# Down-projections of a split-precision FFN: three 256-column matmuls per weight tile, or one of 512 columns and one of 256

## The reference

```python
FFN_HIDDEN = 2816        # 22 chunks of 128
D_FF = 3 * D_MODEL       # 3072: 24 chunks of 128

# first block
gt, up = jnp.split(h @ w_gate_up[i], 2, axis=-1)
f = (jax.nn.silu(gt) * up) @ w_down[i]                        # (256, 2816) @ (2816, 1024)
x = x + rms_norm(f, ffn_post_g[i])

# second block
u = causal_dwconv(jnp.einsum('bsd,df->bsf', h, w_up[l]), ffn_conv_w[l])
gate, up = jnp.split(u, 2, axis=-1)
x = x + jnp.einsum('bsf,fd->bsd', jax.nn.gelu(gate) * up, w_down[l])   # (256, 3072) @ (3072, 1024)
return rms_norm_2(x, final_g)
```

## Time and profile before

| | us |
|---|---|
| median of 3 runs | 949.2 (949.17 to 949.22) |
| the profiled execution, whole time | 949.5 |
| its span, first to last instruction | 947.7 |
| PE busy | 935.1 (99% of the span) |
| PE weight loads (PEld), beside the matmuls | 905.7 (96%) |
| DVE busy | 720.0 (76%) |
| ACT busy | 523.2 (55%) |
| POOL busy | 17.1 (2%) |
| first down-projection on PE | 521.96 to 586.25 |
| second down-projection on PE | 867.63 to 937.68 |

### The profile page before, as it was taken

The page is one execution under the profiler, slowest core; times in us unless marked ns, Lnnn a source line. Parts: engine busy times, 40 slices in busy tenths (PEclk is TensorE's granted clock), DMA queues, the critical chain, the costliest instruction groups (busy, mean ns, idle before and its releaser), DMA issues.

```text
span 947.7 us, 19332 instructions
## 1 busy us (share of the span) xinstructions
PE 935.1 (99%) x7228; PEld 905.7 (96%) x7228; DVE 720.0 (76%) x1297; ACT 523.2 (55%) x871; POOL 17.1 (2%) x27
## 2 busy tenths in 40 slices
PE   9999999999999999999999999999999999999997
PEld 7999999999999999999999999999988999999997
DVE  5999999999999888677767445898615888888432
ACT  5547666777667475555554434577213656656331
POOL 0000000000000000000000000000000000000001
PEclk9999999999999999999999999999999999999999
DMA  7576334544544557256555555346046555555601
GB/s 303 181 247 204 127 120 170 199 154 157 193 130 165 201 197 239 98 189 234 179 186 186 174 184 178 112 158 198 25 154 221 192 185 179 181 187 182 204 0 45
DMA packets 45324, 161.54 MB, mean 170 GB/s; under 512 B 5172, under 2 KB 6360, under 8 KB 45144
## 3 DMA queue, kind: packets, MB, share of 16 engines
q1 hardware_dynamic: 43200, 154.61, 48.5%
q10 hardware_dynamic: 2072, 6.21, 1.9%
HBM read 159.72 MB, written 1.09 MB: 170 GB/s over the span
## 4 chain that ended last, share of the span: by engine, by line
PE 63%; issue 24%; DVE 9%; ACT 2%; DMA 1%; POOL 0%; DVEq 0%; ACTq 0%; SPq 0%; POOLq 0%
PE A L393 11%; PE A L394 10%; PE A L395 10%; PE B L393 5%; PE B L395 5%; PE B L394 5%; PE B L588 5%; PE B L755 3%; DVE w_lo L1191 2%; DVE part L1227 2%; PE B L743 1%; DVE acc L1430 1%; ACT dec L906 1%; PE A L569 1%; DMA raw<-in_weights_dram 1%
## 5 line engine op out<-in xcount | busy, mean ns | idle before, releaser
L1191 DVE TENSOR_TENSOR w_lo<-raw,w_hi 128x1024 fp32r<-128x1024 f32 x257 | 312.8, 1222 | 98.2 <-ACT w_hi L804 95.9
L804 ACT ACTIVATE w_hi<-raw 128x1024 fp32r<-128x1024 f32 x257 | 268.8, 1054 | 134.6 <-PE B L395 75.1
L393 PE MATMUL A<-h_lo,w_hi 128*128 128x256 f32 x1176 | 338.0, 287 | 3.2 <-DVE h_lo L1586 1.6
L394 PE MATMUL A<-h_hi,w_hi 128*128 128x256 f32 x1176 | 332.8, 283 | 0.0
L395 PE MATMUL A<-h_hi,w_lo 128*128 128x256 f32 x1176 | 332.8, 283 | 0.0
L393 PEld LDWEIGHTS A<-h_lo,w_hi 128*128 128x128 f32 x1176 | 225.3, 192 | 6.0 <-issue 3.8
L394 PEld LDWEIGHTS A<-h_hi,w_hi 128*128 128x128 f32 x1176 | 225.5, 192 | 0.2
L395 PEld LDWEIGHTS A<-h_hi,w_lo 128*128 128x128 f32 x1176 | 225.3, 192 | 0.0
L393 PE MATMUL B<-h_lo,w_hi 128*128 128x256 f32 x448 | 128.0, 286 | 0.4 <-DVE h_lo L1196 0.4
L394 PE MATMUL B<-h_hi,w_hi 128*128 128x256 f32 x448 | 126.8, 283 | 0.0
L395 PE MATMUL B<-h_hi,w_lo 128*128 128x256 f32 x448 | 126.8, 283 | 0.0
(11 more groups left out here) (243 smaller groups left out, 1093.8 us busy)
## 6 DMA issues: line engine op xcount, KB each, us to landing
raw<-in_weights_dram SPq DMA_DIRECT2D x290, 512.0 KB, 4.0
csrow<-cs_dram ACTq DMA_DIRECT2D x9, 512.0 KB, 4.2
x<-in_x_dram SPq DMA_DIRECT2D x2, 512.0 KB, 5.1
bd<-in_lru_w_dram ACTq DMA_DIRECT2D x1, 1024.0 KB, 4.8
out_dram<-m_wide SPq DMA_DIRECT2D x5, 128.0 KB, 2.2
out_dram<-m_wide ACTq DMA_DIRECT2D x3, 128.0 KB, 2.3
par<-in_params_dram SPq DMA_DIRECT2D x1, 379.0 KB, 7.3
cst<-in_consts_dram SPq DMA_DIRECT2D x1, 320.0 KB, 7.5
```

Source lines behind the costliest of these rows:

```text
L393: mm(dst, wh, lo, start=first, stop=False, skip_group_check=free)
L394: mm(dst, wh, hi, start=False, stop=False, skip_group_check=free)
L804: F(w_hi[:, s, :], raw[:, s, :], ACT.Copy).then_inc(hi_ready, 1)
L1191: V.tensor_tensor(w_lo[:, s, :], raw[:, s, :], w_hi[:, s, :].bitcast(F32), ALU.subtract).then_inc(lo_ready, 1)
```

## The change

The two halves of the operand lie side by side in one buffer, `hid[:, k, :]` = [lo | hi], 512 columns. For outputs m = 0 to 6 a tile is two matmuls: w_hi on all 512 columns, whose sums with lo land in the left half of a bank and those with hi in the right half, and w_lo on the 256 columns of hi, which adds to the left half. Each of these outputs has a bank of its own, 512 columns of partial sums that have to be added afterwards. Output 7 keeps the three matmuls of 256 columns in the left half of the eighth bank; its right half stays free.

With a bank for each output, the first matmul of each starts the sum, the clearing matmuls go, and the loop of `down_turns` is written out. The banks are taken in the order in which the up-projection's last pairs leave them, with a wait for every second output (`staged` in the first FFN, `pairs_drained` in the second). The waits of PE in the rest, on outputs 0 to 3 before it went on to 4 to 7, go.

The extra addition: in the first FFN, ACT copies the right half to `m_wide` (`half_copied`), DVE adds the left half in place (`m_copied`), and ACT squares the sum. In the second, DVE adds two halves to the residual, one after the other. The norm's scratch columns move from A3 and A2 to banks 1 and 2 of B.

```diff
--- before.py
+++ after.py
@@ -222,8 +222,8 @@
         s3.close()
 
         s4 = ExitStack()
-        hid_hi = sb("hid_hi", [P, KF2, T], F32R, s4)
-        hid_lo = sb("hid_lo", [P, KF2, T], F32R, s4)
+        hid = sb("hid", [P, KF2, 2 * T], F32R, s4)
+        hid_lo, hid_hi = hid[:, :, 0:T], hid[:, :, T:2 * T]
         stage3 = sb("stage3", [P, 2, T], scope=s4)
         s4.close()
 
@@ -279,7 +279,10 @@
 
         DVE_OUT = 5
         out_weighted = stage[:, 0, :], stage[:, 1, :], stage2[:, 0, :]
-        pool_rstd = A[2][:, T:2 * T]
+        pool_rstd = B[:, 2, T:2 * T]
+
+        DOWN_BANKS = [B[:, n, :] for n in (1, 2, 0, 3)] + [A[n][:, :] for n in range(4)]
+        down_sums, down_rstd = B[:, 1, 0:TT], B[:, 1, T:2 * T]
 
         LRU_BANKS = [A[n][:, 0:T] for n in range(3)] + [B[:, n, 0:T] for n in range(4)] + [A[3][:, 0:T]]
         SC_BANKS = [A[0][:, 0:T]] + [B[:, n, 0:T] for n in range(4)] + [A[3][:, 0:T]]
@@ -326,6 +329,7 @@
         lru_tap, sc_ready, lru_ready = sem("lru_tap"), sem("sc_ready"), sem("lru_ready")
         sc_x_used = sem("sc_x_used")
         out_ready, stored = sem("out_ready"), sem("stored")
+        half_copied = sem("half_copied")
         weighted, pool_out = sem("weighted"), sem("pool_out")
         last_scale = sem("last_scale")
 
@@ -661,23 +665,30 @@
             for j in range(UP1_TURNS * 4, KF):
                 ring_pair(j, 0)
 
-            def down_turns(p, turns, operand):
-
-                with pe.Fori(0, turns) as i:
-                    for m in range(KD):
-                        pe.wait_ge(lo_ready, split_order(p + m, i))
-                        if m == 0:
-                            pe.wait_ge(operand_ready, i * 8 + (operand + 8))
-                        for k in range(8):
-                            ins = tile((p + m) % RING, k, hid_hi[:, bass.ds(i * 8 + k, 1), :].rearrange("p a t -> p (a t)"),
-                                       hid_lo[:, bass.ds(i * 8 + k, 1), :].rearrange("p a t -> p (a t)"),
-                                       acc_out(m), False, False, True)
-                        ins.then_inc(pieces_done, 1)
-
-            pe.wait_ge(staged, STAGED_FFN1 + 4 * UP1_TURNS)
-            clear_accumulators()
+            def down_tile(slot, j, k, m, first, last):
+
+                if m == KD - 1:
+                    return tile(slot, j, hid_hi[:, k, :], hid_lo[:, k, :], DOWN_BANKS[m][:, 0:T], first, last, True)
+                wh = w_hi[:, slot, j * P:(j + 1) * P]
+                mm(DOWN_BANKS[m], wh, hid[:, k, :], start=first, stop=False, skip_group_check=True)
+                return mm(DOWN_BANKS[m][:, 0:T], w_lo[:, slot, j * P:(j + 1) * P], hid_hi[:, k, :], start=False, stop=last,
+                          skip_group_check=True)
+
+            def down_turns(p, turns, operand, drained_by_now, drained_n):
+
+                for n in range(turns * KD):
+                    i, m = n // KD, n % KD
+                    pe.wait_ge(lo_ready, split_order(p + n))
+                    if i == 0 and m % 2 == 0:
+                        pe.wait_ge(drained_by_now, drained_n + m // 2)
+                    if m == 0:
+                        pe.wait_ge(operand_ready, i * 8 + (operand + 8))
+                    for k in range(8):
+                        ins = down_tile((p + n) % RING, k, i * 8 + k, m, n < KD and k == 0, False)
+                    ins.then_inc(pieces_done, 1)
+
             done1 = 3 * KD
-            down_turns(DOWN1, 2, done1)
+            down_turns(DOWN1, 2, done1, staged, STAGED_FFN1 + KF - 3)
             for n in range(DOWN1_REST * KD):
                 p = DOWN1 + 2 * KD + n // 8
                 m, k = n // DOWN1_REST, n % DOWN1_REST
@@ -685,13 +696,10 @@
                     pe.wait_ge(lo_ready, split_order(p))
                 if m == 0:
                     pe.wait_ge(operand_ready, done1 + 2 * KD + k + 1)
-                if m >= 4 and k == 0:
-                    pe.wait_ge(m_copied, KD + m - 3)
-                ins = tile(p % RING, n % 8, hid_hi[:, 2 * KD + k, :], hid_lo[:, 2 * KD + k, :], acc_out(m),
-                           False, False, True)
+                ins = down_tile(p % RING, n % 8, 2 * KD + k, m, False, k == DOWN1_REST - 1)
                 if n % 8 == 7:
                     ins.then_inc(pieces_done, 1)
-            spread_residual(5, 13, 4 * KD, A[2][:, :], 2)
+            spread_residual(5, 13, 4 * KD, B[:, 2, :], 2, norm_bank=B[:, 1, :])
 
 
             ops = done1 + KF
@@ -768,21 +776,16 @@
                 for j in range(4):
                     pe.wait_ge(pairs_drained, i * 4 + (KD + j - 3))
                     up2_pair(j, i)
-            pe.wait_ge(pairs_drained, KD + KF2 - 2)
-            clear_accumulators()
-            down_turns(DOWN2, 2, ops + KD)
+            down_turns(DOWN2, 2, ops + KD, pairs_drained, KD + KF2 - 3)
             for m in range(KD):
                 p = DOWN2 + 2 * KD + m
                 pe.wait_ge(lo_ready, split_order(p))
                 if m == 0:
                     pe.wait_ge(operand_ready, ops + KD + KF2)
-                if m >= 4:
-                    pe.wait_ge(x_new, 3 * KD + m - 3)
                 for k in range(8):
-                    ins = tile(p % RING, k, hid_hi[:, 2 * KD + k, :], hid_lo[:, 2 * KD + k, :], acc_out(m), False, False,
-                               True)
+                    ins = down_tile(p % RING, k, 2 * KD + k, m, False, k == 7)
                 ins.then_inc(pieces_done, 1)
-            spread_residual(8, 16, 7 * KD, A[2][:, :], 4, 0)
+            spread_residual(8, 16, 7 * KD, B[:, 2, :], 4, 0, norm_bank=B[:, 1, :])
             for t in range(TT):
                 ins = mm(pool_rstd[:, t * P:(t + 1) * P], scale[:, t:t + 1].to_broadcast([P, P]), ident, start=True, stop=True)
             ins.then_inc(rstd_ready, 1)
@@ -1076,7 +1079,12 @@
                     split_hi(p + LEAD)
 
                 act.wait_ge(pieces_done, down1_done(m))
-                copy_and_square(acc_out(m), m_wide[:, m, :], sq_wide[:, m, 0:T])
+                if m == KD - 1:
+                    copy_and_square(DOWN_BANKS[m][:, 0:T], m_wide[:, m, :], sq_wide[:, m, 0:T])
+                else:
+                    F(m_wide[:, m, :], DOWN_BANKS[m][:, T:2 * T], ACT.Copy).then_inc(half_copied, 1)
+                    act.wait_ge(m_copied, KD + m + 1)
+                    F(sq_wide[:, m, 0:T], m_wide[:, m, :], ACT.Square).then_inc(squares_ready, 1)
 
             act.dma_start(bd[:, :, :, :], lru_w).then_inc(lru_w_loaded, 16)
 
@@ -1665,11 +1673,14 @@
                     split_lo(p + LEAD)
                 if c == 0:
                     lru_rates()
-                if c < KD - 2:
-                    add_square(sq_wide, 4 * KD, c)
-                if c == KD - 3:
+                if c < KD - 1:
+                    dve.wait_ge(half_copied, c + 1)
+                    V.tensor_tensor(m_wide[:, c, :], m_wide[:, c, :], DOWN_BANKS[c][:, 0:T], ALU.add).then_inc(m_copied, 1)
+                if 1 <= c < KD - 1:
+                    add_square(sq_wide, 4 * KD, c - 1)
+                if c == KD - 2:
                     add_squares_up()
-            residual_scaled(14, 13, "ffn_post_g", "norm1_g_2", hi_n, KD, sums, rstd)
+            residual_scaled(14, 13, "ffn_post_g", "norm1_g_2", hi_n, KD, down_sums, down_rstd)
             sum_squares(sq_wide, 5 * KD)
             for p in range(LRUX0 + LEAD, LRUX0 + LEAD + 2):
                 split_lo(p)
@@ -1851,12 +1862,21 @@
             hid2_low(KF2 - 1, 1)
             for p in range(DOWN2, PIECES):
                 split_lo(p + LEAD)
-            add_accumulated(down2_done, 7 * KD)
-            moment_of(17, D, RMS_EPS).then_inc(mean_ready, 1)
+            for m in range(KD):
+                dve.wait_ge(pieces_done, down2_done(m))
+                if m < KD - 1:
+                    after(own.up(V.tensor_tensor(x[:, m, :], x[:, m, :], DOWN_BANKS[m][:, 0:T], ALU.add)))
+                half_ = slice(0, T) if m == KD - 1 else slice(T, 2 * T)
+                V.tensor_tensor(x[:, m, :], x[:, m, :], DOWN_BANKS[m][:, half_], ALU.add).then_inc(x_new, 1)
+                if 1 <= m < KD - 1:
+                    add_square(sq_wide, 7 * KD, m - 1)
+                if m == KD - 2:
+                    add_squares_up()
+            moment_of(17, D, RMS_EPS, down_sums).then_inc(mean_ready, 1)
             dve.wait_ge(rstd_ready, 16)
             dve.wait_ge(x_new, 4 * KD)
             for c in range(DVE_OUT):
-                V.scalar_tensor_tensor(m_wide[:, c, :], x[:, c, :], col("final_g_2", c), rstd, ALU.mult,
+                V.scalar_tensor_tensor(m_wide[:, c, :], x[:, c, :], col("final_g_2", c), down_rstd, ALU.mult,
                                        ALU.mult).then_inc(out_ready, 1)
 
 
```

## The result

The changed kernel takes **951.5 us** (median of 8 runs, 950.9 to 952.9) against 949.2 for the kernel before (8 runs, 949.1 to 949.4): a ratio of 1.0024, 95% interval 1.0015 to 1.0033. It is slower by 2.3 us, where 3.2 us less were forecast, and lies outside the range given. The profiled execution took 950.9, with a span of 949.1 (before: 947.7).

A forecast was written before the change was run, and what follows sets the result against it. PE's matmul stream, busy 99% of the span, was taken as the bound. Tiles -3.2, clearing matmuls -1.86, wait at the first down-projection's end +1.86 made -3.2 us: 949.2 to 946.0, range 943.5 to 949.4.

The forecast's parts named there:

- The stream of tiles: Both down-projections: a tile takes 350 ns instead of 360, so 322 tiles save 3.2 us.
- Both rivals on the stream: Wide matmul at 240 ns: stream saves nothing, 949.2 us, chance 0.15; at 216 ns: saves far more, 941.5 us, chance 0.15.
- The clearing matmuls: Ahead of both down-projections: four zero matmuls go each time, saving 1.86 us, with no wait for banks expected.
- The end of the second down-projection: DVE's extra additions there cost nothing, with a margin of 1.2 us.
- I cost this at nothing: First down-projection: ACT's next split may come 1 to 1.5 us late behind its square; priced at no cost.
- the ring of pieces: First down-projection: splits made six to eight pieces ahead of PE, 2.8 us a piece, cover late splits.
- ACT wakes at 586.44: End of first down-projection: ACT starts copying output 6 then, taking 0.38 us; start of the reckoning of the join.
- The wait at the end: End of first down-projection: PE waits for DVE's join of the squares, 1.86 us lost, bounds 1.5 to 2.5.
- The common report of outputs 6 and 7: End of first down-projection: the last piece reports both together, so the join comes late; 1.86 us lost.
- The path at the end costs more: Rival: a split or ACT's order delays the join further, or delayed splits reach PE; 947 to 948 us, chance 0.03.
- The slow rival: Each change between 512 and 256 columns in a tile costs 50 ns, adding 12.9 us: 962 us, chance 0.05.

The follow-up runs named there:

- experiment 8: Experiment 5's kernel with the 512-column matmul cut into two of 256 again, in the same banks: 948.5 us.
- experiment 6: Experiment 5's kernel with the four matmuls on zeros put back ahead of each down-projection: 947.3 us.
- experiment 2: Changed kernel with the new form in the second down-projection alone, the first as in the kernel before: 946.8 us, ratio 0.9973 to before.
- experiment 3: Changed kernel with DVE's block of small operations (lru_rates) moved ahead of its splits of the first down-projection's pieces: 948.6 us, ratio 0.9988 to before.
- experiment 10: Changed kernel with only a semaphore added, reporting output 6 of the first down-projection at its own sixth tile: 951.6 us, ratio 1.0025 to before.
- experiment 4: Experiment 3's kernel with DVE's addition of an output placed ahead of the split of the piece: 947.8 us, ratio 0.9981 to before.
- experiment 1: Changed kernel with 18 matmuls on zeros between the first down-projection's last tile and the wait for the joined squares: 948.7 us, ratio 0.9992 to before.
- experiment 9: Experiment 5's kernel with the first down-projection's last split moved behind output 6's square on ACT and the join on DVE: 944.8 us, ratio 0.9951 to before.
- experiment 7: Experiment 4's kernel with 9 matmuls on zeros between the first down-projection's last tile and the wait for the join: 946.5 us.
- experiments 5: Experiment 4's kernel with output 6 of the first down-projection reported to ACT by its own semaphore at its sixth tile: 945.6 us, ratio 0.9963 to before.

## Why the prediction was wrong, point by point

- **The stream of tiles: right.** The pair was forecast at 350 ns and takes that. 322 tiles were to save 3.2 us; cutting the merge out again costs 3.0 (experiment 8). Both rivals on the stream, 240 ns and 216 for the wide matmul, fell. The Trainium skill's page "TensorE: Matmul & The Clock Gate", section "Back-to-back issue gap", gives 2.5 ns beside the columns for each matmul, as the gap of isolated ones at the full clock; by it the saving would have been an estimated 0.8 us. The fp32r matmuls of this kernel do not agree: the merge gave 9.3 ns a tile.
- **The clearing matmuls: right.** 1.86 forecast, 1.7 measured (experiment 6), with no wait for banks.
- **The end of the second down-projection: right.** It costs nothing; the second alone gives 2.6 of the 2.6 forecast (experiment 2).
- **"I cost this at nothing": the step that failed.** Of ACT and DVE in the first down-projection I wrote that ACT's square may find DVE in a split, that the next split would be late, and that the ring of pieces covers it. The pieces were indeed never late. But I followed only the splits and asked whether PE would wait for weights. I did not follow the other thing queued on the same two engines, the sums of squares, which PE waits for at the end. ACT's square behind DVE's addition, and DVE's addition behind a split that ACT starts after its square, made a ring of 2.99 us a turn against 2.8 of PE, and the small block on DVE, 3 us long and known from the order of its program, stood right in front of it. It cost 2.07 us of the gap (experiment 3). Then "ACT wakes at 586.44" took for granted that ACT was free. It was a whole output behind.
- **The wait at the end: right place, wrong cause.** The join was late, as forecast, but 4.2 us instead of 1.86, and by the queue. The common report of outputs 6 and 7, on which the 1.86 rested, does not decide in the changed kernel (experiment 10). Where ACT and DVE are free in time, in experiment 4, it does, and measures 1.88.
- **The clock: a term that was missing.** I counted the wait as its own length. Behind 4.07 us of idle PE the clock fell, for 2.6 us more (2.8 by the medians of experiment 1, 2.4 by its span). Even the 1.86 that I had forecast would have cost some 1.4 beyond its length in the median: experiment 4 is 3.0 above experiment 9, of which experiment 7, with the clock held up, has 1.6.
- **The rivals.** "The path at the end costs more" had 0.03 and 947 to 948. "A split or ACT's order delays the join further" is what happened, but I let it cost 1 or 2 us, and gave it next to nothing since I had priced its cause at nothing. The slow rival with its 50 ns a change of form did not occur.

With wait and clock in it the sum reads 949.2 - 3.2 - 1.9 + 4.2 + 2.6 = 950.9, 0.6 under the median of 951.5. That the profiled execution took just 950.9 is in part chance: it is the shortest of eight, and 0.35 of it was gained before the first down-projection. Executions with this gap spread over 2 us.

## What to carry to other kernels

Where a change makes two engines hand an item back and forth (copy here, add there, square here again), write down one whole turn of it with everything that stands between in both queues, and compare it with the pace of the producer: if the turn is longer, every delay is kept to the end. Put the short instruction that another engine waits for ahead of the long one that has slack, and keep unrelated blocks away from the point where the hand-over starts. A wait of PE has to be priced with the clock it may lose; where it can't be removed, matmuls on zeros of the same length were here the cheaper way to spend it (2.8 us in experiment 1, 1.4 in experiment 7).

## What the runs showed of the hardware

- An fp32r matmul of 256 columns with its own weight load has a pitch of 120 ns, one of 512 columns on real data 230 over both down-projections, where the zero matmuls had 232.5. Per column 512 are cheaper, by about 10 ns for each matmul saved. The records of plain fp32 matmuls of 256 columns, two for each matmul, have a pitch of 216.
- An idle time of PE of 1.73 us (experiment 4) was followed by a stretch at a mean granted clock of 0.60, one of 2.00 us (experiment 3) by 0.62, one of 0.65 us (experiment 8) by 0.77. It was not so each time: two idle times of 0.8 us were followed by 1.00, and one execution each of experiments 3 and 4 had 1.00 over its whole span. With PE kept on zeros through the same wait the clock stayed at 1.00. The next matmuls after such a gap are the ones that pay: 7.4 to 9.0 us for what takes 6.45. The fall comes not in the wait but 0.5 to 2.2 us after PE has gone on (changed kernel and experiment 8).
- Kernels with a gap of 2 us or more spread over 1.4 to 2.0 us from run to run, those with one of 0.9 to 1.1 (experiments 5, 6, 8) over 1.1 to 1.6, and those with none or a filled one over 0.2 to 0.5.
